# A mixer's context columns normed, split and multiplied ahead of its latent columns

## What is computed

```python
# end of the first block: latents only
x = x + gate * rms(swiglu(h_l, w_gate, w_up, w_down))     # D_FF = 2816
# start of the second block, which has a context of its own (ctx_2)
h_l = modulate(rmsnorm(x, norm1_g[l]), mod_l[:, 0], mod_l[:, 1])
h_c = modulate(rmsnorm(ctx_2, norm1_g[l]), mod_c[0], mod_c[1])
z_c = h_c @ w_in
z_l = h_l @ w_in
```

## Time and profile before

| What | us |
|---|---|
| Median of three runs | 2471.03 |
| Lowest, highest run | 2469.13, 2473.78 |
| Span of the profiled execution | 2467.0 |
| TensorE busy in it | 2298.7 |
| VectorE busy | 1488.3 |
| ScalarE busy | 1079.4 |
| Down rows of `ffn1.up` end | at 1334.2 |
| First matmul of `mla.in` | at 1349.6 |

### The profile page before, as it was taken

The page is one execution under the profiler, slowest core; times in us unless marked ns, Lnnn a source line. Parts: engine busy times, 40 slices in busy tenths (PEclk is TensorE's granted clock), DMA queues, the critical chain, the costliest instruction groups (busy, mean ns, idle before and its releaser), DMA issues.

```text
span 2467.0 us, 35275 instructions
## 1 busy us (share of the span) xinstructions
PE 2298.7 (93%) x14782; PEld 1829.4 (74%) x14782; DVE 1488.3 (60%) x2374; ACT 1079.4 (44%) x1824; POOL 130.4 (5%) x174
## 2 busy tenths in 40 slices
PE   6978898999998999988998988989999999999999
PEld 3844466888886777777998863447888888879999
DVE  6447846565566377875456325555566565996454
ACT  4344445222234466655455335654332334435543
POOL 0001100000000000000000002100200100000110
PEclk9998999999998999998999999999999999999999
DMA  7165552444422465434653223432444434434553
GB/s 274 69 252 198 212 178 88 146 145 151 151 106 77 137 205 171 137 139 143 195 178 114 103 90 120 156 135 90 157 161 138 154 111 189 181 136 157 188 189 120
DMA packets 173295, 372.47 MB, mean 151 GB/s; under 512 B 7376, under 2 KB 99792, under 8 KB 158800
## 3 DMA queue, kind: packets, MB, share of 16 engines
q1 hardware_dynamic: 173136, 370.21, 43.2%
HBM read 339.74 MB, written 30.44 MB: 150 GB/s over the span
## 4 chain that ended last, share of the span: by engine, by line
PE 78%; DVE 11%; ACT 6%; DMA 3%; issue 2%; POOL 0%; SPq 0%; DVEq 0%; ACTq 0%; POOLq 0%
PE ps L169 77%; DVE sb_R L200 3%; ACT sb_R L252 2%; DMA sb_slot<-mod_w 1%; DVE sb_H L200 1%; ACT sb_R L258 1%; DVE sb_R L229 1%; ACT L245 1%; PE ps L179 1%; DVE sb_WP L200 1%; DMA sb_slot<-even_w_in 1%; DVE sb_X L217 1%; DVE sb_R L214 1%; ACT sb_RS L252 0%; DVE sb_slot L200 0%
## 5 line engine op out<-in xcount | busy, mean ns | idle before, releaser
L169 PE MATMUL ps<-sb_HP,sb_WP 128*128 128x512 f32 (+1 forms) x5712 | 1077.7, 350 | 30.8 <-DVE sb_HP L200 25.9
L169 PEld LDWEIGHTS ps<-sb_HP,sb_WP 128*128 128x128 f32 x5712 | 918.6, 192 | 176.1 <-DVE sb_HP L200 24.6
L200 DVE TENSOR_TENSOR sb_WP<-sb_slot,sb_WP 128x1024 fp32r<-128x1024 f32 x380 | 468.7, 1239 | 576.7 <-ACT sb_WP L258 576.2
L258 ACT ACTIVATE sb_WP<-sb_slot 128x1024 fp32r<-128x1024 f32 x380 | 399.3, 1056 | 715.3 <-PE ps L169 692.8
L169 PE MATMUL ps<-sb_XP,sb_WP 128*128 128x256 f32 (+1 forms) x2976 | 497.3, 330 | 1.7 <-issue 1.4
L169 PEld LDWEIGHTS ps<-sb_XP,sb_WP 128*128 128x128 f32 x2976 | 445.0, 190 | 53.2 <-issue 1.6
L200 DVE TENSOR_TENSOR sb_R<-sb_R 128x256 f32<-128x256 f32 (+4 forms) x411 | 201.4, 526 | 13.6 <-ACT sb_R L252 10.7
L169 PE MATMUL ps<-sb_R 128*32 128x64 f32 (+7 forms) x1768 | 159.4, 286 | 25.6 <-DVE sb_R L200 5.9
L169 PEld LDWEIGHTS ps<-sb_R 128*32 128x32 f32 (+3 forms) x1768 | 113.0, 152 | 63.8 <-issue 34.4
L252 ACT ACTIVATE sb_R<-ps 128x512 f32<-128x512 f32 (+1 forms) x208 | 99.6, 513 | 87.7 <-PE ps L169 83.4
L200 POOL TENSOR_TENSOR sb_R<-sb_R 128x512 f32<-128x512 f32 (+1 forms) x82 | 85.6, 1069 | 811.3 <-ACT sb_R L252 586.1
(11 more groups left out here) (152 smaller groups left out, 1858.6 us busy)
## 6 DMA issues: line engine op xcount, KB each, us to landing
sb_slot<-mlp_w SPq DMA_DIRECT2D x32, 2048.0 KB, 8.9
sb_slot<-mod_w SPq DMA_DIRECT2D x22, 2048.0 KB, 8.7
sb_R<-ada_w SPq DMA_DIRECT2D x12, 2048.0 KB, 7.6
sb_slot<-ada_w SPq DMA_DIRECT2D x24, 1024.0 KB, 4.9
sb_slot<-ffn_w_gate SPq DMA_DIRECT2D x22, 1024.0 KB, 5.5
sb_slot<-ffn_w_up SPq DMA_DIRECT2D x22, 1024.0 KB, 8.1
sb_slot<-ffn_w_down SPq DMA_DIRECT2D x10, 2048.0 KB, 7.7
sb_slot<-odd_w_in SPq DMA_DIRECT2D x32, 512.0 KB, 7.2
```

Of the source, the lines that this page charges most:

```text
L169: return self.e.matmul(out, w, x, start=start, stop=stop, skip_group_check=True)
L200: return BLANK if self.e is None else self.e.tensor_tensor(out, a, b, op)
L258: return self.e.activation(out, a, ACT.Copy) if scale is None else self.e.activation(out, a, ACT.Copy, scale=scale)
```

## The change

- **Context sums.** `Down.pe` of `ffn1` calls `context_pe` between down rows 9 and 10. The sums go to the second half of PSUM bank 0, into which output group 0 also accumulates. In row 10, group 0 comes last and waits until the context's logarithm has read the bank.
- **Context norm.** `context_act` and the new `context_dve` run beside rows 10 to 18: root, multiply, scale and shift, high part, low part of the eight context tiles. They go into `HP` columns 0 to 255. The latents' half goes through an offset (`self.off`) into columns 256 to 511, and the latents' `Norm` of this stage now handles 256 columns only.
- **Weight pieces.** The mixer's pieces 2 and 3 are split after the down rows and before `Resid.act` and `Resid.dve`. Piece 0 is split after the gates and piece 1 after the root on ScalarE, after the last tile on VectorE. `begun` takes them out of `flow_act` and `flow_dve`. With `four`, the loop ahead leaves out piece 3, and slot 0 is given free at piece 1.
- **First block.** `context_first_pe` takes four banks (4 to 7), runs k = 4, 5, 6, 7, 0, 1, 2, 3 for the context columns, puts the eight sums of the latents' norm behind the sixth (four), the seventh (three) and the eighth (one) of them, then runs k = 0 to 7 for the latent columns.
- **Down loads.** `down_loads` gets a last load of two blocks. For the 22 blocks of `ffn1` the old rule gives the same list: 4, 4, 4, 4, 4, 2.

```diff
-    def context_pe(self, pe, ps):
+    def context_pe(self, pe):
...
-            i = pe.mm(ps[:, TC:T], self.p.c("ones"), self.p.H[:, t, 0:TC], t == 0, t == KT - 1)
+            i = pe.mm(self.p.ps[0][:, TC:T], self.p.c("ones"), self.p.H[:, t, 0:TC], False, t == KT - 1)
...
+    def context_dve(self, dve):
+        p, dve = self.p, dve.on(self.stage)
+        for _ in range(10):
+            yield
+        self.mods.wait_co(dve, self.j)
+        dve.wait_ge("crstd")
+        for t in range(KT + 1):
+            if t < KT:
+                sc, sh = self.coeffs(t, 1)
+                h = p.H[:, t, 0:TC]
+                dve.mul(h, p.X[:, t, 0:TC], p.RS[:, 0:TC]).then_inc(*dve.sig("cxn", t))
+                dve.wait_ge("cxn", t)
+                dve.ts(h, h, sc, ALU.mult, sh, ALU.add).then_inc(*dve.sig("ch", t))
+            if t:
+                hp = p.HP[:, :, t - 1, 0:TC]
+                dve.wait_ge("chi", t - 1)
+                dve.sub(hp[:, 1], p.H[:, t - 1, 0:TC], hp[:, 0].bitcast(F32)).then_inc(*dve.sig("chp", t - 1))
+            yield
...
         for k in range(self.kt):
-            self.row_pe(pe, k, next(pieces))
+            hold = amid if k == 10 else None
+            self.row_pe(pe, k, next(pieces), tuple(range(KT)) if hold is None else (1, 2, 3, 4, 5, 6, 7, 0), hold)
+            if amid is not None and k == 9:
+                amid.context_pe(pe)
...
             self.downs[c].act(e, ahead, ready, self.end_act(act) if self.down.c == c else ())
+            if self.resid.context is not None:
+                for x in (2, 3):
+                    self.resid.ahead.act_part(act.on(self.resid.ahead.name), x)
         self.resid.act(act)
...
+    def context_first_pe(self, e, pieces):
...
+        bs = [e.take() for _ in range(4)]
+        ws = [p.wp(next(pieces)) for _ in range(4)]
+        sums = self.norm.sums_pe(e)
+        for n, (y, k) in enumerate((y, 2 * y + z) for y in (2, 3, 0, 1) for z in range(2)):
+            e.wait_ge("w", y)
+            e.wait_ge("chp", k)
+            for a, (_, ps) in enumerate(bs):
+                c = 512 * (k % 2) + 128 * a
+                e.mm3(ps[:, 0:TC], [z[:, c:c + 128] for z in ws[y]], p.hp(k, TC), n == 0, False)
+            for _ in steps(sums, {5: 4, 6: 3}.get(n, 0)):
+                pass
+        at_once(sums)
+        for k in range(KT):
+            y = k // 2
+            e.wait_ge("hp", k)
+            for a, (b, ps) in enumerate(bs):
+                c = 512 * (k % 2) + 128 * a
+                x = [p.HP[:, z, k, TC:T] for z in range(2)]
+                i = e.mm3(ps[:, TC:T], [z[:, c:c + 128] for z in ws[y]], x, False, k == KT - 1)
...
-    ffn1.resid.context = mla.proj.norm
+    ffn1.resid.context, ffn1.resid.ahead = mla.proj.norm, mla.proj.pieces
+    mla.proj.pieces.begun = mla.proj.pieces.four = True
```

## The result

The kernel after takes 2476.83 us (median of 7 runs, 2476.00 to 2483.07), the kernel before 2470.93 (7 runs, 2468.93 to 2473.78). The ratio is 1.0033, with a 95% interval of 1.0023 to 1.0043. It counts all runs; by the medians alone it would be 1.0024, since two of the seven runs took 2482.5 and 2483.1 us. So the change makes the kernel slower by 5.9 us (medians) to 8 us (all runs), and the interval lies clear of the 0.2% that counted as no change. The time lies in the predicted range; the side that the prediction called likeliest, no change, is wrong.

The account below looks back on a forecast made before the run. TensorE, busy 93% of the span, was taken as the bound, so only the seam counted: 41.95 us after against 38.7 before, +3.2, added to the median 2471.0 gave 2474.2 us; range 2468.0 to 2477.5.

Parts of the forecast that it names:

- The seam: From the end of ffn1.up's down rows to the end of mla.in's first block: 38.7 us before, 41.95 after.
- (1): Sign behind down row 9: sixteen ones-matmul instructions in 3.5 us, and the last row's end later by that.
- (2): Sign on ScalarE: first mixer weight copy just after w_in lands, ended by a DMA, the squares behind it.
- (3): Sign on TensorE: idle of about 5 us ahead of the output norm's sums, about 2.9 ahead of the latent half.
- (4): Sign in the first block's context half: granted clock of 0.50.
- the sum: Seam terms added up: 41.95 us after against 38.7 before, +3.2 us, added to the median.
- (5): Sign on VectorE: under 2.89 us of work in each of down rows 10 to 18.
- The first rival: Weight pieces 2 and 3 hidden in ScalarE's idle before the squares, TensorE waiting 1.0 us: −2.6, 2468.4 us; chance 20%.
- the second clock loss: Half clock after the 2.9 us idle ahead of the latent half: 0 to 1.7 us, taken as 1.1.
- The second rival: VectorE cannot keep up in down rows 10 to 18, last down piece and load late: +6.2, 2477.2 us; chance 20%.
- The split's price: Mixer's first block as 192 matmuls of 256 columns, not 96 of 512: 23.1 instead of 21.9 us, +1.2.
- The step that failed: Outside the seam: dense TensorE streams the other engines do not bound, so only the seam can change the time.

## Why the prediction was right and wrong

**The seam was right, step by step.** (1) The context's sums took 3.62 us behind row 9, and the last row ended at 1337.9, where 1337.7 was predicted (the profiled execution was 0.2 us late already at the start of `ffn1`). (2) The load was issued at 1328.7 (predicted 1328.6), ScalarE's copies began at 1336.7 (1336.4), the squares at 1338.65 (1338.4), the additions at 1340.50. (3) TensorE idled 5.33 us (5.2) and 2.79 us (2.9). (4) The granted clock was 0.54 behind both, from 1343.5 to 1346.2 and from 1363.4 to 1366.7. Against the kernel with the early load, whose clock stays up, the two cost 1.1 and 1.35 us, where the sum had 1.6 and 1.1. (5) VectorE stayed under 2.89 us in the rows: it idles 0.20 us ahead of most weight pieces, the very 0.2 that the prediction left. The sum was +3.2, and +3.3 was measured. The first rival (pieces hidden) was wrong as to this kernel, but right about its worth: with the load early the seam was 3.4 us shorter than before, where the rival had −2.6; it had kept the second clock loss (1.1), which did not come either. The second rival (VectorE over 2.89) did not occur.

**The split's price** was 1.2 by the spacing of the rows and 1.1 in the kernel that has nothing else of the change. The 0.2 us that followed from the Trainium skill, "TensorE: Matmul & The Clock Gate", Back-to-back issue gap, whose formula is for isolated matmuls, is not what this chip showed for these pairs of weight load and matmul: 0.120 us at 256 columns and 0.228 at 512. (The 21.9 us of the prediction are start to start, 1372.90 to 1394.81; the row has 21.7.)

**The step that failed** stands at the end of the first paragraph: "the other engines do not bound those stretches, so only the seam can change the time". It took the time after the seam for untouched, because no instruction there is another. The late stage lost 3.8 us all the same. The loss was in a term that the sum did not have: 96 matmuls and 96 weight loads more, priced at their 1.2 us, also shift the places at which TensorE's code is loaded. That the step failed by this is shown by the kernel with the narrower matmuls alone, which loses 2.8 us there, and by the 66 instructions that took the loss away. The rows that could have warned were in the trace of the kernel before: five issue idles of 1.0 to 1.5 us, 6.3 in all, in one stage of small matmuls. They show that TensorE catches up with its code there. They do not tell which shift costs and which gains, so the sum would have got a range (the nine kernels gave −0.5 to +3.8), and the chance of "slower" would have had to be much higher: with +3.3 from the seam, more than 1.6 us of such a loss takes it over the 0.2%.

**A smaller slip**: the prediction called the 4.0 us between the profiled span and the median of the runs "what lies around the span". The profiled execution of the kernel after took 2476.3 us with a span of 2474.3, so only 2.0 lie around it. In the kernel before, the rest was the scatter of runs. It did not matter, as the sum was a difference added to the median.

**What stays open.** Why the load of code comes late in some positions (in the kernel after it begins 1.6 us after TensorE has stopped) and in time in others is not shown. Each late stage was seen in one profiled execution per kernel, while the timed runs of one kernel scatter by up to 10 us (2466.3 to 2476.4 with 384 more). Nor was it tried whether the small matmuls can be given their code in another way.

## What to carry over

A load that a moved step needs must be looked at together with everything that stands behind this step in its engine's program. Two copies of 1 us ahead of the squares, with their wait for the load, cost 4.3 us of idle on TensorE and 2.4 of clock behind it; placing them behind the squares gave half of this back, loading into a slot that is free sooner all of it. Where the trace shows "issue" idle on TensorE in a stage of small matmuls, an edit anywhere ahead that alters the number of TensorE's instructions can move that stage by several us: measure it there apart from the edit, with a few dummy or split instructions more, before the edit is judged.

## What was not expected of the hardware

TensorE's code arrives in packets of 16 KB, and its stalls stand on a grid of 256 matmuls and weight loads. In and just behind the runs of matmuls of 64 columns it stalled 1.0 to 1.8 us one to five times in a late stage, and once 3.1 to 4.3 us in the kernels with 192, 324 and 384 instructions more. Behind the 3.9 us stall of the kernel after the granted clock was 0.50 for the next 5 us; behind the 3.6 us stall of the kernel with the early load it stayed at 1.00 (2222.9 to 2226.0).

An idle of 2.8 us ahead of the latent half was followed by 0.54 of the clock in the kernel after, and by full clock in the kernel with the early load. The window view of the kernel after, and behind it that of the kernel with the early load:

```profile
1363.40:1366.70 3.30, 3.30 (x16) 3.30 (x17) 3.15 (x10) 2.37 (x6) 0.00 (x0) 0.54 0.02 5
```

```profile
1358.00:1361.00 3.00, 1.60 (x13) 1.60 (x14) 2.91 (x9) 2.16 (x5) 0.00 (x0) 1.00 0.02 9
```

The length of the idle is the same in both (2.79 and 2.80 us). What TensorE did before it differs: in the kernel after it had idled 5.3 us some 20 us earlier and had run at half clock behind that. So had the kernel with 258 more and the late load, and its idle of 2.80 us was followed by half clock too. But in the kernel with the pieces behind, which also had a half clock earlier, the idle of 2.79 us was followed by full clock, so an earlier loss does not settle it, and the idle's length alone does not tell whether the clock falls. This stays open.
